# Sum of squares behind the first weight slice, and a head in another order: a float32 hybrid trunk on one core

## The chip, the cores and the metric

One core of one Trainium2 chip runs the kernel. The metric is device time in microseconds of one launch that computes both layers. The kernel before takes 2107.37 us (median of 3 runs, 2106.95 to 2107.5).

## What is computed

Each of two layers normalizes x, projects it once, mixes the columns in three branches, merges these with gates and adds a last projection to x. Cut to what matters here:

```
for i in range(DEPTH):                                  # DEPTH = 2
    h = rmsnorm(x, norm_w[i])                           # x: 256 tokens x 2048
    proj = h @ w_in[i]                                  # 2048 x 13840
    (u, s5_gate, z, xbc, dt_raw, q, k, v, att_gate, merge_logits) = split(proj)
    ...                                                 # S5, SSD and attention branches
    branches = einsum('blnw,nwd->blnd', ys, w_branch[i])
    merged = sum(sigmoid(merge_logits) * branches)
    x = x + merged @ w_out[i]

def rmsnorm(t, w):
    y = t * rsqrt(mean(t * t, axis=-1) + 1e-6)
    return y * w
```

## The kernel before, in words

x lies transposed: 16 tiles of 128 channels by 256 tokens. The scale of the norm over the channels, norm_w, is multiplied in before the projection, and the scale over the tokens, called rstd, after it, when a result leaves PSUM. So the products need the scaled x only, and rstd is first needed by the tensor operation that empties the bank of slice 0.

**Products.** All large weights come as a stream of 148 slices per layer, each 128 x 2048 float32 (1 MB). Slice n is loaded by SP into one of two buffers `raw`, rounded by ACT to `w_hi` (helper `hi`, L580), and DVE takes the rest, `w_lo` = raw - w_hi (helper `lo`, L860). x is split likewise into `h_hi` and `h_lo`. PE computes a slice as 48 products (`pair`, and three calls at L1464 to L1466: w_hi x h_lo, w_lo x h_hi, w_hi x h_hi, for 16 tiles of channels). `raw`, `w_hi`, `w_lo` and the PSUM banks `mm` have two places each: slice n + 2 can be rounded only when the products of slice n are done (semaphore `pair_done`), and slice n + 2 can be multiplied only when DVE has emptied the bank of slice n.

**Order of work.** Every engine has its own program in the order in which it is written (blocks `sync` for SP, `gpsimd` for POOL, `scalar` for ACT, `vector` for DVE, `tensor` for PE), and semaphores join them. In the head SP loads x in four quarters of 512 KB (L344), norm_w (L346), the first two slices (L348), the constants (L349), and copies x to the output (L350). ACT squares the 16 tiles (L597), POOL adds the squares up in `ssum` (L416), and DVE multiplies the tiles by norm_w (L888). Then ACT and DVE split slices 0 and 1.

**Start of a layer.** ACT makes the four quarters of `h_hi` (L606, marks xhi0 to xhi3), DVE those of `h_lo` (xlo0 to xlo3). In `first(0)` PE waits for `ssum` and multiplies it by a matrix of ones (L1502, mark "ss"), which gives the sum over the channels in bank b4; only then it starts slice 0. DVE turns b4 into mean plus eps behind xlo0 (L900, mark "rs_v"), ACT takes Ln (L590) and Exp (L592) of it (`inv_sqrt`), and DVE improves the result by one Newton step of four operations (`newton`, ending in mark "rs_n4"). Behind slice 0 PE waits for rs_n4 and transposes rstd (L1522, mark "rtok"). In the loop over n of DVE (0 to 15) each turn waits for the products of slice n, empties the bank (mark "in" and n), and splits slice n + 2. Turn 0 ends with `s5_angles`, a chain of 14 small operations, whose first needs "s5_dt" of ACT, and which ACT's Tanh (L619) waits for before it rounds slice 3. In the second layer the squares and the scaled tiles come from the loop over the slices of w_out (squares L845, sums on POOL L559, scaling L1450).

Of the kernel before, what the change touches and what calls it, by code (L numbers as in the profile page):

```python
# [10 lines left out]
ALU = mybir.AluOpType  # L11
# [13 lines left out]
EPS = 1e-6  # L25
# [107 lines left out]
def program(nc, x, norm_w, params, consts, bdense, stream, xs_out, order):  # L133

    with ExitStack() as ctx:
# [204 lines left out]

        @block.sync
        def _(e):
            for q in range(4):
                e.dma_start(proj[:, 4 * q:4 * q + 4, :], x[:, 4 * q:4 * q + 4, :]).then_inc(x_in[q], 16)  # L344
                if q == 0:
                    e.dma_start(nw[:, 0:DEPTH, :], norm_w).then_inc(nw_in, 16)  # L346
            for j in range(RAW):
                e.dma_start(raw[:, j, :], stream[j]).then_inc(landed[j], 16)  # L348
            e.dma_start(cst[:], consts).then_inc(const_in, 16)  # L349
            e.dma_start(xs_out[0], x).then_inc(x_copied, 16)  # L350
            W = Where(e)

            def load(nb, j):

                e.wait_ge(lo_done, nb + (j + 1 + RAW))
                e.dma_start(raw[:, j % RAW, :], stream[nb + (j + RAW)]).then_inc(landed[j % RAW], 16)

            with e.Fori(0, DEPTH) as L:
                with e.Fori(0, N_GATE // 2 + 1) as I:
                    nb = e.snap(L * N_LAYER + I * 2)  # L360
                    for j in range(2):
                        load(nb, j)

                with e.Fori(0, 4) as I:
                    nb = e.snap(L * N_LAYER + N_GATE + I * 12)
                    g0 = e.snap(I * 12)

                    for c in range(2):
                        W.b[MA] = e.snap((L * 8 + I * 2 + (c + 2)) * MA.n)
                        for t in range(6):  # L370
                            s = 6 * c + t
                            W.wait(MA, f"gate{t}")
                            e.dma_start(gscr[g0 + s], gt[:, s % 4, :]).then_inc(spilled[s % 4], 16)
                            load(nb, s + 2)
                with e.Fori(0, (N_BR - N_SG) // 2 - 1) as I:
                    nb = e.snap(L * N_LAYER + (N_SG + 2) + I * 2)
                    for j in range(2):
                        load(nb, j)

                for s in range(4):  # L380
                    e.wait_ge(spilled[s], e.snap((L * 12 + 13) * 16))
                W.settle()
                with e.Fori(0, (N_OUT - N_BR) // 2) as I:
                    nb = e.snap(L * N_LAYER + N_BR + I * 2)
                    for j in range(2):
                        load(nb, j)
                        e.dma_start(gin[:, j % 2], gscr.rearrange("(n a) p t -> n p a t", a=2)[I * 2 + j]).then_inc(gate_in[j % 2], 16)
                with e.Fori(0, (N_LAYER - N_OUT) // 2) as I:
                    nb = e.snap(L * N_LAYER + N_OUT + I * 2)
                    for j in range(2):  # L390
                        load(nb, j)
            e.wait_ge(x_out, (DEPTH + 1) * 64)
            e.wait_ge(x_copied, 16)
# [170 lines left out]
        def _(e):  # L564
# [29 lines left out]
            for m in range(KT):  # L594
                if m % 4 == 0:
                    e.wait_ge(x_in[m // 4], 16)
                e.activation(proj[:, 16 + m, :], proj[:, m, :], ACT.Square).then_inc(x_sq, 1)  # L597
            hi(0, 0)
            hi(0, 1)
            with e.Fori(0, DEPTH) as L:  # L600
                W.layer(L)

# [1 line left out]
                for q in range(4):  # L604
                    e.wait_ge(x_w, e.snap(L * 16 + (4 * q + 4)))
                    LA.mark(e.activation(h_hi[:, 4 * q:4 * q + 4, :], proj[:, 32 + 4 * q:36 + 4 * q, :], ACT.Copy), f"xhi{q}")  # L606
                inv_sqrt(LA, "rs", rstd[:], sv[:, 1, :], sv[:, 0, :], lambda: W.wait(LV, "rs_v"))

                nb = start(L, 0)
                for n in range(16):  # L610
                    hi(nb, n + 2)
                    if n == 0:
                        e.wait_ge(par_in, e.snap((L + 1) * 16))
                        LA.mark(e.activation(sp[:, 0, :], PR("log_dt", 0, ST), ACT.Exp), "s5_dt")
                        LA.mark(e.activation(sd[:, 6, 0:16], PR("a_log", 0, 16), ACT.Exp), "exp_a")
                        LA.mark(e.activation(wdt_hi[:], PR("w_dt", 0, KT * 16).rearrange("p (k c) -> p k c", k=KT), ACT.Copy), "wdt_hi")
                        LA.mark(e.activation(bgh[:], PR("b_glu", 0, BT), ACT.Copy, scale=0.5), "bgh")
                        W.wait(LV, "s5_ax")
                        LA.mark(e.activation(sp[:, 2, :], sp[:, 1, :], ACT.Tanh, scale=0.5), "s5_tanh")  # L619
                    if n == 1:  # L620
                        W.wait(LV, "turn_abs")
                        LA.mark(e.activation(sp[:, 5, :], sp[:, 3, :], ACT.Sin, scale=TWO_PI / 2), "s5_sin")
                        LA.mark(e.activation(sp[:, 6, :], sp[:, 4, :], ACT.Sin, scale=-TWO_PI / 2, bias=C("half_pi")), "s5_cos")
                    if n == 5:
                        W.wait(LV, "dt_abs")
                        LA.mark(e.activation(sd[:, 2, :], sd[:, 1, :], ACT.Exp, scale=-1.0), "dt_exp")
                    if n == 6:
                        W.wait(LV, "k_raw")
                        LA.mark(e.activation(kk[:, 0, :], kt[:].rearrange("p a b -> p (a b)"), ACT.Square), "k_sq")
                    if 4 <= n < 8:  # L630
                        t = n - 4
                        W.wait(LV, f"bc_conv{t}_3")
                        if t:
                            W.wait(LV, f"bc_silu{t - 1}")
                        LA.mark(e.activation(bt[:], kk[:, 2, 0:TOK] if t % 2 == 0 else kk[:, 2, TOK:], ACT.Tanh, scale=0.5), f"bc_tanh{t}")
                    if n == 8:
                        inv_sqrt(LA, "k", kk[:, 0, :], kk[:, 1, :], kk[:, 3, :], lambda: W.wait(LV, "k_v"))
                    if n == 13:
                        W.wait(LV, "k_fin")
                        e.dma_start(kscr.rearrange("a p t -> p a t"), kt[:]).then_inc(k_out, 16)  # L640
                        LA.mark(e.activation(small[:, 12:13], C("half_pi"), ACT.Copy), "prep_end")
# [208 lines left out]
        def _(e):  # L850
# [34 lines left out]
            for m in range(KT):  # L885
                if m % 4 == 0:
                    e.wait_ge(x_in[m // 4], 16)
                e.tensor_scalar(proj[:, 32 + m, :], proj[:, m, :], nw[:, 0, m:m + 1], None, ALU.mult).then_inc(x_w, 1)  # L888
            lo(0, 0)
            lo(0, 1)  # L890
            with e.Fori(0, DEPTH) as L:
                W.layer(L)
                e.wait_ge(x_w, e.snap((L + 1) * 16))
                for q in range(4):
                    W.wait(LA, f"xhi{q}")
                    LV.mark(tt_(h_lo[:, 4 * q:4 * q + 4, :], proj[:, 32 + 4 * q:36 + 4 * q, :],
                                h_hi[:, 4 * q:4 * q + 4, :].bitcast(F32), ALU.subtract), f"xlo{q}")
                    if q == 0:
                        W.wait(LP, "ss")
                        LV.mark(e.tensor_scalar(sv[:, 0, :], b4[:, 0:TOK], 1.0 / D_MODEL, EPS, ALU.mult, ALU.add), "rs_v")  # L900
                newton(LV, "rs", rstd[:], sv[:, 1, :], sv[:, 0, :])


                count = [0]

# [114 lines left out]
                for n in range(16):  # L1020
                    if n == 8:
                        e.wait_ge(x_out, e.snap((L + 1) * 64))
                        W.settle()
                    e.wait_ge(pair_done, nb + (n + 3))
                    bank = mm[:, n % 2, 0:256]
                    if n < 4:
                        LV.mark(tt_(proj[:, BC + n, :], bank, rstd[:], ALU.mult), f"in{n}")
# [9 lines left out]
                    if n == 4:  # L1037
                        W.wait(LP, "dt_t")
                        LV.mark(tt_(sv[0:16, 0, :], b6[0:16, 0:256], rstd[0:16, :], ALU.mult), "dt_s")
                    lo(nb, n + 2)  # L1040
                    if n == 0:
                        s5_angles()
                    if n == 1:
                        W.wait(LP, "rtok")
                        chain(e.tensor_copy(rtok[:], b5[:, 0:2]), "rtok")
                        W.wait(LA, "wdt_hi")
                        LV.mark(tt_(wdt_lo[:], PR("w_dt", 0, KT * 16).rearrange("p (k c) -> p k c", k=KT), wdt_hi[:].bitcast(F32),
                                    ALU.subtract), "wdt_lo")
# [407 lines left out]
        def _(e):  # L1456
# [33 lines left out]
                                    xhi[:, k, :], xlo[:, k, :], k == 0, k == BT - 1)  # L1490
                ins.then_inc(pair_done, 1)

            e.wait_ge(const_in, 16)
            with e.Fori(0, DEPTH) as L:
                W.layer(L)

                xs = e.snap(L * 17 + 18)

                def first(q):
                    if q == 0:  # L1500
                        e.wait_ge(x_sum, xs)
                        LP.mark(e.matmul(b4[:, 0:TOK], C("ones"), ssum[:], start=True, stop=True), "ss")  # L1502
                    W.wait(LV, f"xlo{q}")


                nb = e.snap(L * N_LAYER)
                for n in range(16):
                    if n in (6, 7):
                        e.wait_ge(lo_done, nb + (n + 1 + RAW))
                        for t in range(2):  # L1510
# [5 lines left out]
                    else:  # L1516
                        pair(nb, n, first if n == 0 else None)
                    if n == 0:

                        W.wait(LV, "rs_n4")  # L1520
                        for t in range(2):
# [328 lines left out]
```

## Time and profile before

| | before |
|---|---|
| median of 3 runs | 2107.37 us |
| span of the profiled execution, first to last instruction | 2106.1 us |
| what a run has around that span (difference of the two) | 1.3 us |
| TensorE matmul busy | 2024.8 us, 96% |
| VectorE busy | 1610.8 us, 76% |
| ScalarE busy | 1040.8 us, 49% |
| GpSimd busy | 669.4 us, 32% |
| mean granted TensorE clock | 0.995 of full |

The time of a run covers one launch. The profile is of one execution, and its span goes from the first instruction to the last. Busy time counts data work of an engine, not its waits. PE is the multiplying part of TensorE, PEld its loading of weights; DVE is VectorE, ACT ScalarE, POOL GpSimd, SP SyncE. A granted clock of 1.00 is 2.4 GHz, one of 0.50 is 1.2 GHz.

### The profile page before, as it was taken

Reading aid. Unit: us, or ns where it says so; the run is one execution under the profiler, and the core shown is the slowest. Engines: PE = TensorE matmul, PEld = TensorE weight load, DVE = VectorE, ACT = ScalarE, POOL = GpSimd, SP = SyncE. Lnnn points to the kernel's source line nnn. Section 1 sums busy time; section 2 is a strip of 40 time slices with the busy share of each in tenths; the row PEclk is TensorE's granted clock in tenths of the full one; section 3 lists DMA queues with packets and bytes.
Section 4 is the critical chain, followed back from the end, with each engine's and each line's share of the span. In section 5 each row is a group of like instructions: output and inputs, shape, how many; then the busy total and the mean of one; then the engine's idle time right before and its main releaser. Section 6 shows DMA issues by size and latency. Waiting matters only on the chain.

```text
span 2106.1 us, 45313 instructions
## 1 busy us (share of the span) xinstructions
PE 2024.8 (96%) x15852; PEld 1921.2 (91%) x15852; DVE 1610.8 (76%) x2366; ACT 1040.8 (49%) x1389; POOL 669.4 (32%) x816
## 2 busy tenths in 40 slices
PE   5999999999999999999989999999999999999998
PEld 5999999988888999999989899999888889999998
DVE  6658899888898867766567688889898978586755
ACT  5334334657665645333343344447565666453333
POOL 3045666434353000002300656665343330000033
PEclk9999999999999999999999999999999999999999
DMA  6344444434344445665543444444443444466654
GB/s 245 128 169 143 159 151 151 160 141 156 138 159 142 155 156 218 231 225 205 201 163 127 167 154 155 146 166 142 148 164 142 138 156 143 161 243 227 231 195 179
DMA packets 74125, 356.98 MB, mean 170 GB/s; under 512 B 8048, under 2 KB 33136, under 8 KB 35440
## 3 DMA queue, kind: packets, MB, share of 16 engines
q1 hardware_dynamic: 70704, 342.93, 45.5%
q0 software_dynamic: 1600, 7.85, 1.0%
q10 hardware_dynamic: 1696, 4.72, 0.6%
q8 instruction: 56, 0.92, 0.2%
q14 instruction: 69, 0.57, 0.1%
HBM read 338.17 MB, written 19.40 MB: 170 GB/s over the span
## 4 chain that ended last, share of the span: by engine, by line
PE 83%; DVE 6%; issue 5%; ACT 2%; POOL 2%; DVEq 0%; DMA 0%; ACTq 0%; POOLq 0%; SPq 0%
PE mm L1464 24%; PE mm L1465 23%; PE mm L1466 23%; PE bs L1569 3%; PE b L1557 3%; DVE w_lo L860 1%; DVE prod L864 1%; PE by L1624 1%; ACT w_hi L580 1%; DVE xc L1005 1%; PE b L1615 1%; PE b L1636 1%; PE b L1635 1%; POOL ssum L416 1%; PE b L1642 0%
## 5 line engine op out<-in xcount | busy, mean ns | idle before, releaser
L1464 PE MATMUL mm<-h_lo,w_hi 128*128 128x256 f32 x3776 | 1103.9, 292 | 3.5 <-DVE h_lo L864 3.5
L1465 PE MATMUL mm<-h_hi,w_lo 128*128 128x256 f32 x3776 | 1070.7, 284 | 0.0
L1466 PE MATMUL mm<-h_hi,w_hi 128*128 128x256 f32 x3776 | 1070.2, 283 | 0.0
L580 ACT ACTIVATE w_hi<-raw 128x2048 fp32r<-128x2048 f32 x298 | 569.6, 1911 | 792.1 <-PE mm L1466 775.5
L860 DVE TENSOR_TENSOR w_lo<-raw,w_hi 128x2048 fp32r<-128x2048 f32 x298 | 696.7, 2338 | 160.1 <-ACT w_hi L580 152.2
L1464 PEld LDWEIGHTS mm<-h_lo,w_hi 128*128 128x128 f32 x3776 | 725.4, 192 | 35.0 <-issue 27.4
L1465 PEld LDWEIGHTS mm<-h_hi,w_lo 128*128 128x128 f32 x3776 | 725.8, 192 | 3.9 <-issue 1.0
L1466 PEld LDWEIGHTS mm<-h_hi,w_hi 128*128 128x128 f32 x3776 | 725.3, 192 | 0.0
L1464 PE MATMUL mm<-ys,w_hi 128*128 128x256 f32 x768 | 217.5, 283 | 2.2 <-DVE w_lo L860 2.2
L1465 PE MATMUL mm<-ys,w_lo 128*128 128x256 f32 x768 | 217.3, 283 | 0.0
L1466 PE MATMUL mm<-ys,w_hi 128*128 128x256 f32 x768 | 217.3, 283 | 0.0
L559 POOL TENSOR_TENSOR ssum<-ssum,proj 128x256 f32<-128x256 f32 x32 | 72.7, 2271 | 398.3 <-ACT proj L845 398.3
L1464 PEld LDWEIGHTS mm<-ys,w_hi 128*128 128x128 f32 x768 | 147.4, 192 | 2.6 <-DVE w_lo L860 2.6
L1466 PEld LDWEIGHTS mm<-ys,w_hi 128*128 128x128 f32 x768 | 147.4, 192 | 0.0
L1465 PEld LDWEIGHTS mm<-ys,w_lo 128*128 128x128 f32 x768 | 147.4, 192 | 0.0
L864 DVE TENSOR_TENSOR prod<-prod,prod 128x256 f32<-128x256 f32 x256 | 121.8, 515 | 1.7
L437 POOL TENSOR_SCALAR tA<-cst,cur 128x256 f32<-128x256 f32 x64 | 65.3, 1021 | 148.7 <-ACT tab L651 143.5
L468 POOL COPY cz<-par 64x64 f32 x64 | 47.6, 744 | 194.2 <-PE bs L1569 185.7
L864 DVE TENSOR_TENSOR proj<-mm,rstd 128x256 f32 (+1 forms) x104 | 43.6, 419 | 74.4 <-PE mm L1466 73.5
L864 DVE TENSOR_TENSOR prod<-wst,tab 128x512 f32<-128x512 f32 x128 | 89.3, 738 | 0.5
L549 POOL DMA_DIRECT2D x_old<-out x2 | 1.2, 610 | 277.8 <-PE mm L1466 277.8
L448 POOL TENSOR_TENSOR tB<-tB,tA 128x256 f32<-128x256 f32 x64 | 85.0, 1329 | 5.3
(268 smaller groups left out, 2576.4 us busy)
## 6 DMA issues: line engine op xcount, KB each, us to landing
raw<-in_stream SPq DMA_DIRECT2D x298, 1024.0 KB, 4.8
gscr<-gt SPq DMA_DIRECT2D x96, 128.0 KB, 1.7
gin<-gscr SPq DMA_DIRECT2D x48, 256.0 KB, 4.9
x_old<-out POOLq DMA_DIRECT2D x2, 2048.0 KB, 10.6
out<-proj ACTq DMA_DIRECT2D x8, 512.0 KB, 3.7
proj<-in_x SPq DMA_DIRECT2D x4, 512.0 KB, 6.9
par<-in_params POOLq DMA_DIRECT2D x2, 759.0 KB, 5.4
cst<-in_consts SPq DMA_DIRECT2D x1, 1029.0 KB, 12.8
```

The costliest lines, as they stand in the source:

```text
L437: SGp.mark(e.tensor_scalar(tA[:], C("iota"), cur5[:, j:1 + j], ROUND, ALU.mult, ALU.add), f"ta{j}")
L448: SGp.mark(e.tensor_tensor(tB[:], tB[:], tA[:], ALU.add), f"tf{j}")
L468: SGp.mark(e.tensor_copy(cz[rows, :, r, 16 * g:16 * g + 16], par[rows, bass.ds(i * 64 + PP[nm][0], 64)].rearrange("p (j h) -> p j h", j=4) ...
L559: e.tensor_tensor(ssum[:], ssum[:], proj[:, bass.ds(I * 4 + (16 + j), 1), :].rearrange("p a b -> p (a b)"), ALU.add).then_inc(x_sum, 1)
L580: e.activation(w_hi[:, j % SPLIT, :], raw[:, j % RAW, :], ACT.Copy).then_inc(hi_done, 1)
L860: e.tensor_tensor(w_lo[:, j % SPLIT, :], raw[:, j % RAW, :], w_hi[:, j % SPLIT, :].bitcast(F32), ALU.subtract).then_inc(lo_done, 1)
L864: return e.tensor_tensor(out, a, b, op)
L1464: e.matmul(out, whi, xlo, start=start, stop=False)
L1465: e.matmul(out, wlo, xhi, start=False, stop=False)
L1466: return e.matmul(out, whi, xhi, start=False, stop=stop)
L1557: ins = e.matmul(b4[:, r * 256:r * 256 + 256], bz[:, r, 2 * j:2 * j + 2, :].rearrange("p a b -> p (a b)"), proj[:, bass.ds(I + (U + more), ...
L1569: ins = e.matmul(ps_s5[32 * j:32 * j + 32, :], cz[:, j, r, :], prod[:, j % 2, r, :], start=r == 0, stop=r == 1)
```

## The change

Four things move; no operation on data is added or dropped.

- On PE the product "ss", with its waits for the constants and for `ssum`, goes from ahead of slice 0 to behind it, and "rtok" from behind slice 0 to behind slice 1. Ahead of slice 2 PE now waits for "in0", the emptying of the bank of slice 0.
- On DVE "rs_v", the Newton step and in0 stand in turn 0 behind the split of slice 2; the copy of rtok goes from turn 1 to turn 2.
- On ACT Ln and Exp stand behind the rounding of slice 2.
- In the head SP loads norm_w first, and slices 0 and 1 behind quarters 0 and 1 of x. ACT rounds slice 0 behind tile 3 and slice 1 behind tile 7; DVE takes the rest of slice 0 behind tile 7 and of slice 1 behind tile 15.

```diff
 @block.sync
+            e.dma_start(nw[:, 0:DEPTH, :], norm_w).then_inc(nw_in, 16)
             for q in range(4):
                 e.dma_start(proj[:, 4 * q:4 * q + 4, :], x[:, 4 * q:4 * q + 4, :]).then_inc(x_in[q], 16)
-                if q == 0:
-                    e.dma_start(nw[:, 0:DEPTH, :], norm_w).then_inc(nw_in, 16)
-            for j in range(RAW):
-                e.dma_start(raw[:, j, :], stream[j]).then_inc(landed[j], 16)
+                if q < RAW:
+                    e.dma_start(raw[:, q, :], stream[q]).then_inc(landed[q], 16)
 @block.scalar
                 e.activation(proj[:, 16 + m, :], proj[:, m, :], ACT.Square).then_inc(x_sq, 1)
-            hi(0, 0)
-            hi(0, 1)
+                if m == 3:
+                    hi(0, 0)
+                if m == 7:
+                    hi(0, 1)
...
-                inv_sqrt(LA, "rs", rstd[:], sv[:, 1, :], sv[:, 0, :], lambda: W.wait(LV, "rs_v"))
                 for n in range(16):
                     hi(nb, n + 2)
                     if n == 0:
+                        inv_sqrt(LA, "rs", rstd[:], sv[:, 1, :], sv[:, 0, :], lambda: W.wait(LV, "rs_v"))
                         e.wait_ge(par_in, e.snap((L + 1) * 16))
 @block.vector
                 e.tensor_scalar(proj[:, 32 + m, :], proj[:, m, :], nw[:, 0, m:m + 1], None, ALU.mult).then_inc(x_w, 1)
-            lo(0, 0)
+                if m == 7:
+                    lo(0, 0)
             lo(0, 1)
...
-                    if q == 0:
-                        W.wait(LP, "ss")
-                        LV.mark(e.tensor_scalar(sv[:, 0, :], b4[:, 0:TOK], 1.0 / D_MODEL, EPS, ALU.mult, ALU.add), "rs_v")
-                newton(LV, "rs", rstd[:], sv[:, 1, :], sv[:, 0, :])
...
                     e.wait_ge(pair_done, nb + (n + 3))
+                    if n == 0:
+                        lo(nb, n + 2)
+                        W.wait(LP, "ss")
+                        LV.mark(e.tensor_scalar(sv[:, 0, :], b4[:, 0:TOK], 1.0 / D_MODEL, EPS, ALU.mult, ALU.add), "rs_v")
+                        newton(LV, "rs", rstd[:], sv[:, 1, :], sv[:, 0, :])
...
-                    lo(nb, n + 2)
+                    if n:
+                        lo(nb, n + 2)
                     if n == 0:
                         s5_angles()
-                    if n == 1:
+                    if n == 2:
                         W.wait(LP, "rtok")
                         chain(e.tensor_copy(rtok[:], b5[:, 0:2]), "rtok")
+                    if n == 1:
                         W.wait(LA, "wdt_hi")
 @block.tensor
-            e.wait_ge(const_in, 16)
...
                 def first(q):
-                    if q == 0:
-                        e.wait_ge(x_sum, xs)
-                        LP.mark(e.matmul(b4[:, 0:TOK], C("ones"), ssum[:], start=True, stop=True), "ss")
                     W.wait(LV, f"xlo{q}")
                 for n in range(16):
+                    if n == 2:
+                        W.wait(LV, "in0")
...
                     if n == 0:
+                        e.wait_ge(const_in, 16)
+                        e.wait_ge(x_sum, xs)
+                        LP.mark(e.matmul(b4[:, 0:TOK], C("ones"), ssum[:], start=True, stop=True), "ss")
+                    if n == 1:
                         W.wait(LV, "rs_n4")
```

How the instructions stand now: the start of a layer on ACT before, from the last quarter of h_hi (L606) to the rounding of slice 2 (L580). L590 is Ln and L592 Exp, each behind a table load.

```order
L606 ACTIVATE h_hi<-proj 128x1024
L331 ISA
L590 ACT_TABLE_LOAD
L590 ACTIVATE sv<-sv 128x256
L331 ISA
L592 ACT_TABLE_LOAD
L592 ACTIVATE rstd<-sv 128x256
L578 ISA
L579 REGISTER_ALU
L580 ACTIVATE w_hi<-raw 128x2048
```

The same place on ACT in the changed kernel, whose lines are L607, L579, L589 and L591:

```order
L607 ACTIVATE h_hi<-proj 128x1024
L577 ISA
L578 REGISTER_ALU
L579 ACTIVATE w_hi<-raw 128x2048
L331 ISA
L589 ACT_TABLE_LOAD
L589 ACTIVATE sv<-sv 128x256
L331 ISA
L591 ACT_TABLE_LOAD
L591 ACTIVATE rstd<-sv 128x256
```

The rounding of slice 2 now stands ahead of Ln, both table loads and Exp.

The same place on DVE in the changed kernel, from the last quarter of h_lo to the emptying of the bank of slice 0. L861 is the rest of slice 2, L1025 is rs_v, the four rows behind it are the Newton step, and the last is in0.

```order
L865 TENSOR_TENSOR h_lo<-proj,h_hi 128x1024
L1021 ISA
L861 TENSOR_TENSOR w_lo<-raw,w_hi 128x2048
L331 ISA
L1025 TENSOR_SCALAR sv<-b 128x256
L331 REGISTER_ALU
L865 TENSOR_TENSOR sv<-rstd 128x256
...
L865 TENSOR_TENSOR sv<-sv 128x256
...
L877 TENSOR_SCALAR sv<-sv 128x256
...
L865 TENSOR_TENSOR rstd<-rstd,sv 128x256
...
L865 TENSOR_TENSOR proj<-mm,rstd 128x256
```

Before, rs_v stood behind the first quarter of h_lo, the Newton step behind the last, then in0, and the rest of slice 2 last.

## Rows read from the trace of the kernel before

**Rows 1.** The page, part 1: an engine's busy us, share, instructions.

```profile
PE 2024.8 (96%) x15852; PEld 1921.2 (91%) x15852; DVE 1610.8 (76%) x2366; ACT 1040.8 (49%) x1389; POOL 669.4 (32%) x816
```

**Rows 2.** Waits of PE over the span: us in total, times, longest us.

```profile
PE b L1502 <- POOL ssum L416: 25.3, 1, 25.3
...
PE b L1676 <- DVE xc L1284: 10.1, 6, 2.0
PE b L1557 <- POOL bz L460: 5.8, 2, 2.9
PE b L1502 <- POOL ssum L559: 4.9, 1, 4.9
```

**Rows 3.** Head: SP's issues (start us, us), then the last quarter's transfer (us to landing).

```profile
1.79 1.38 SPq L344 DMA_DIRECT2D proj<-in_x  x3
```

```profile
proj<-in_x SPq DMA_DIRECT2D x1, 512.0 KB, 8.1
```

**Rows 4.** Timeline of ACT, 27 to 40 us: start us, us, instruction.

```profile
27.42 1.28 ACT L592 ACT_TABLE_LOAD   x1
28.72 0.42 ACT L592 ACTIVATE rstd<-sv 128x256 f32<-128x256 f32 x1
33.33 1.91 ACT L580 ACTIVATE w_hi<-raw 128x2048 fp32r<-128x2048 f32 x1 [4.20 <-PE mm L1466]
...
39.53 1.91 ACT L580 ACTIVATE w_hi<-raw 128x2048 fp32r<-128x2048 f32 x1 [1.59 <-PE mm L1466]
```

**Rows 5.** Timeline of DVE, 8 to 41 us.

```profile
8.30 5.59 DVE L888 TENSOR_SCALAR proj<-proj,nw 128x256 f32<-128x256 f32 x12 [1.27 <-DMA proj<-in_x]
...
20.29 1.74 DVE L864 TENSOR_TENSOR h_lo<-proj,h_hi 128x1024 fp32r<-128x1024 f32 x1
26.53 0.43 DVE L900 TENSOR_SCALAR sv<-b 128x256 f32<-128x256 f32 x1 [4.49 <-PE b L1502]
...
30.27 0.42 DVE L864 TENSOR_TENSOR sv<-rstd 128x256 f32<-128x256 f32 x1
...
31.51 0.42 DVE L864 TENSOR_TENSOR rstd<-rstd,sv 128x256 f32<-128x256 f32 x1
...
35.28 2.29 DVE L860 TENSOR_TENSOR w_lo<-raw,w_hi 128x2048 fp32r<-128x2048 f32 x1 [1.52 <-ACT w_hi L580]
37.49 0.41 DVE L864 TENSOR_TENSOR sp<-par,sp 128x32 f32<-128x32 f32 x2
...
40.50 0.42 DVE L864 TENSOR_TENSOR proj<-mm,rstd 128x256 f32<-128x256 f32 x1
```

**Rows 6.** POOL: all 16 adds of the head, and one beside w_lo.

```profile
5.73 19.49 POOL L416 TENSOR_TENSOR ssum<-ssum,proj 128x256 f32<-128x256 f32 x16 [4.11 <-ACT proj L597]
```

```profile
15.49 2.72 POOL L416 TENSOR_TENSOR ssum<-ssum,proj 128x256 f32<-128x256 f32 x1
```

**Rows 7.** Timeline of PE around slice 0; last, a product of the chain (start, us).

```profile
25.27 1.22 PE L1502 MATMUL b<-ssum,cst 128*128 128x256 f32 x2 [25.27 <-POOL ssum L416]
25.93 0.78 PE L1464 MATMUL mm<-h_lo,w_hi 128*128 128x256 f32 x1
...
33.13 0.50 PE L1522 MATMUL b<-cst,rstd 128*128 128x1 f32 x4
```

```profile
28.84 0.14 PE mm L1466
```

**Rows 8.** Start of the second layer, timelines of ACT and PE.

```profile
1064.49 3.90 ACT L606 ACTIVATE h_hi<-proj 128x1024 fp32r<-128x1024 f32 x4 [4.12 <-issue]
```

```profile
1066.86 0.58 PE L1464 MATMUL mm<-h_lo,w_hi 128*128 128x256 f32 x1 [2.61 <-DVE h_lo L864]
...
1069.58 0.39 PE L1464 MATMUL mm<-h_lo,w_hi 128*128 128x256 f32 x1
```

**Rows 9.** Stretches: us, PE busy (instructions), granted clock, DMA share, GB/s.

```profile
148.50:151.50 3.00, 3.00 (x14) 0.50 0.19 27
476.00:479.00 3.00, 3.00 (x16) 0.50 0.71 300
```

## The prediction, made before the changed kernel was run

> **What bounds the kernel now.** The page's first part shows PE busy for 2024.8 of 2106.1 us [rows 1], so only what makes PE idle, or multiply slowly, can change the time by much. I therefore read PE's waits next. The longest is the start: PE sits for 25.3 us until POOL has summed the squares of the first layer, and at the second layer it waits 4.9 us for the same sum [rows 2]. Then I read the timelines of the head and of the boundary between the layers, engine by engine, to see what else would hold slice 0 if that sum did not. In the head DVE had the first quarter of h_lo at 22.03 us (20.29 + 1.74) [rows 5], so 3.9 us of the wait up to 25.93, where slice 0 starts [rows 7], are the sum's. At the second layer slice 0 starts at 1066.86 and was released by h_lo, itself held by ACT, which began h_hi only at 1064.49 behind 4.1 us that are put down to issue [rows 8]. There the wait for the sum is covered: ss could vanish and slice 0 would start no earlier.
>
> **Term 1, the head.** In the new order 2.0 MB have to land before quarter 1 of x is there (quarter 0, slice 0, quarter 1). The same 2.0 MB were the four quarters before; the last was issued at about 2.7 (the end of 1.79 + 1.38, less its own 0.4) and landed 8.1 later, at 10.8 [rows 3]. From there DVE is busy without a gap. Its scaling takes 5.59 / 12 = 0.47 us a tile beside POOL's adds, w_lo 2.29, the first quarter of h_lo 1.74 [rows 5]: 4 x 0.47 + 2.29 + 8 x 0.47 + 2.29 + 1.74 = 11.95, less some 0.25 where neighbours overlap, gives 22.5. ACT keeps ahead of it: a rounding takes 1.91 [rows 4], and by my count slice 0, whose data are in with the first 1.5 MB, is rounded by about 11.5, and slice 1 by about 15.4. So the new order of the head brings nothing by itself, slice 0 can start at 22.5 instead of 25.93, and all that is won is the wait for the sum.
>
> A part of it is lost again. Of what PE did from 25.27 until 28.84 everything ran slowly, one product in 0.21 us, and 0.12 from then on [rows 7]. The product ss, some 1.2 us, no longer takes the first part of these 3.6 us, so slice 0 has about 17 slow products instead of 11: its products take 17 x 0.21 + 31 x 0.12 = 7.3 us, 7.5 with the filling of the pipe, and slice 0 ends at 30.0. It ended at 33.3 (ACT is released at 33.33, [rows 4]). **Gain 3.3 us.** From below I take 2.3 (each of the two w_lo and the quarter held 0.3 longer by POOL), from above 4.8: the four scalings between transfers at 0.35 each, and quarter 1 a microsecond earlier.
>
> Is the sum ready when slice 0 ends? POOL took 19.49 us for 16 adds, and one beside w_lo took 2.72 [rows 6]. In the new order it does 4 by about 10, waits for the next squares until 11.9, and has four long adds beside two w_lo and four quarters of h_lo: I come to 28.5, under 30.0. If it is later by up to 2 us nothing follows, as the next term shows.
>
> **Term 2, the stall before slice 2, in each layer.** This is what the change adds. Let slice 0 end at 0. Before, slice 2 followed at 39.53 - 33.33 = 6.2 [rows 4]: rtok and slice 1, whose bank and weights were ready. Now its bank must be emptied by in0, and in0 stands at the end of a chain that starts with the rounding of slice 2. Step by step, each with its duration: the rounding 1.91; w_lo of slice 2 starts 1.95 behind the rounding's start (35.28 against 33.33) and the next operation 2.21 behind that [rows 4, 5], so rs_v starts at 4.2 and ends at 4.6, while ss (0.6 us at the full clock) is long done; Ln takes 0.43, and table load and Exp 29.14 - 27.42 = 1.72 [rows 4], to 6.8; the table load for Ln stands ahead of its wait and hides behind w_lo; the Newton step takes 31.93 - 30.27 = 1.66 [rows 5], to 8.5; in0 0.42, to 8.95; the first product starts at 9.1 with its pipe empty. PE meanwhile has ss and slice 1, 6.4 us, then sits for 2.1, does rtok (0.35) when rs_n4 is there, and sits again. So slice 2 starts 9.1 - 6.2 = **2.9 us later, in each layer**. What is queued behind the wait is only slice 2 itself, so the delay passes on whole.
>
> Here a row and a rule differ. Exp starts 1.30 us behind the start of its table load, with nothing between [rows 4]. The Trainium skill (ScalarE: Activation LUTs, What ACT_TABLE_LOAD costs) puts every change of table at 2.66 us, load and drain; with that the chain would be 1.4 us longer in each layer. The row decides; the rule is a rival below.
>
> What is late next: DVE does s5_angles behind in0, 3.0 us (37.49 to 40.50), and only then in1 and w_lo of slice 3 [rows 5]. That gives 8.95 + 3.0 + 0.4 + 2.3 = 14.65, and slice 2 ends at 9.1 + 5.76 = 14.9. So slice 3 is not held, by 0.2 us.
>
> **Term 3, the second layer.** Slice 0 starts at 1066.86 as before, since h_lo is what it waits for. Its products were slow until about 1069.8, 2.9 us [rows 8]; without ss at 1063 that can be as in the head, up to 3.6, which costs 0 to 0.35. I take **0.1 us**.
>
> **Term 4, the clock.** The stalls of term 2 can also cost clock. PE's two waits of some 2.9 us for bz were both followed by about 3.4 us at 0.50 (148.5 to 151.5 shows the first). Of the six waits for xc, of up to 2.0 us, one was: behind it PE stood at 0.50 in 476 to 479, and did 16 products in 3 us [rows 2, 9]. That costs 3.4 / 2 = 1.7 us each time. My stalls have 2.1 us without work, rtok, and 0.25 more, between these cases. Six in ten each, I estimate; so one fall in two stalls is likeliest: **1.7 us**.
>
> The rest costs nothing: the load of norm_w ahead of x is 0.4 us of issue inside the transfers that quarter 1 waits for; the constants' transfer is long in; rtok's copy moved to turn 2 is 0.15 us on DVE, with slice 6 its first reader.
>
> **Sum.** -3.3 + 2 x 2.9 + 0.1 + 1.7 = +4.3 us on the profiled 2106.1. The median of the runs is 1.3 above that span and takes the same difference: 2107.4 + 4.3 = 2111.7. A difference of under 0.2%, 4.2 us, is what measurement can't tell from none, so the forecast sits on the edge of it.
>
> **Rivals.**
> - The clock falls in neither stall: +2.6, 2110.0, no measurable change. For it: five of six waits of about 1.5 to 2.0 us left the clock alone. Against: the stall is nearer 2.5.
> - It falls in both: +6.0, 2113.4. The two stalls are alike, and so were the two for bz, which both fell.
> - The head wins more, 4.8 us, with stalls of 2.8 and no fall: +0.8 + 0.1, 2108.3. For it: transfers could land earlier in another order. Against: DVE has 12 us of work in a row that no transfer holds. To come out faster at all, the head has to win 5.9, thus slice 0 has to start before 20; nothing of DVE's rows allows that.
> - The chain of term 2 is longer than its operations, by 1.4 us a layer: an engine that changes its table waits for its pipe to drain. Then slice 2 is 4.3 late, and the time 4.3 + 2.8 = +7.1, 2114.5. This is what the rule above would make of it. Against: the 1.30 us of the row.
> - The change does not do what it says, in that PE waits for the sum all the same: ssum later than slice 0's end by over 2.1 us, thus past 32. Each microsecond beyond adds one. It needs three more long adds than I count.
>
> **How the numbers follow.** Forecast (one fall) 0.42; none 0.19; both 0.28; the head wins more 0.06; the longer chain 0.02; the late sum 0.03. Each has some 1.5 us of its own, from the phase of the clock, from fetches of instructions (the 4.1 us put down to issue may move), and from terms 1 and 2. So above +4.2 lie half of the first, an eighth of the second, nearly all of the third and the last two: slower 0.52. Below -4.2 almost nothing: 0.02. Within 0.2%: 0.46. The range goes from +0.4, which takes in the rival of the head, to +8.0: 2107.8 to 2115.4.
>
> **What would show it.** In the changed profile: slice 0 starts at 22 to 23 us without a wait for ssum; POOL's last add ends before 30; ahead of rtok, and again ahead of slice 2, PE waits for DVE's rstd and proj, 2 to 2.7 us together in each layer; slice 2 starts 9.1 us behind the end of slice 0 in place of 6.2; slice 0 of the second layer starts at h_lo, 2.61 us of wait with ss gone becoming a long one; a granted clock of 0.50 for 3.4 us behind one of the stalls. A slice 0 that starts before 21, or a stall under 1.5 us, would make the prediction wrong.

## The result, and the profile after

The changed kernel takes 2113.84 us (median of 6 runs, 2113.38 to 2114.55) against 2107.40 before (6 runs): ratio 1.0032, 95% interval 1.0022 to 1.0042. It is slower by 6.4 us, of which 4.3 were forecast. The profiled execution has a span of 2112.3 us, 6.2 above that of before.

The page, part 1, and PE's waits of the changed kernel answer to [rows 1, 2]:

```profile
PE 2029.7 (96%) x15852; PEld 1926.7 (91%) x15852; DVE 1611.0 (76%) x2366; ACT 1040.4 (49%) x1389; POOL 670.4 (32%) x816
```

```profile
PE mm L1468 <- DVE h_lo L865: 31.4, 4, 21.8
...
PE b L1683 <- DVE xc L1288: 10.1, 6, 1.9
PE b L1564 <- POOL bz L459: 5.7, 2, 2.8
PE b L1529 <- DVE rstd L865: 4.5, 2, 2.5
```

PE has the same 15852 instructions and is busy for 4.9 us more: slower products, not more of them. The two waits for ssum of 25.3 and 4.9 us are gone, waits for h_lo stand in their place, 21.8 us at the start and 8.7 at the second layer, and new are two for DVE's rstd, 4.5 us together. What follows are the timelines of ACT, DVE and PE around the first two slices [rows 4, 5, 7]:

```profile
29.14 1.91 ACT L579 ACTIVATE w_hi<-raw 128x2048 fp32r<-128x2048 f32 x1 [8.50 <-PE mm L1470]
31.07 1.28 ACT L589 ACT_TABLE_LOAD   x1
33.82 0.42 ACT L589 ACTIVATE sv<-sv 128x256 f32<-128x256 f32 x1 [1.46 <-DVE sv L1025]
34.25 1.28 ACT L591 ACT_TABLE_LOAD   x1
35.55 0.42 ACT L591 ACTIVATE rstd<-sv 128x256 f32<-128x256 f32 x1
...
45.81 1.92 ACT L579 ACTIVATE w_hi<-raw 128x2048 fp32r<-128x2048 f32 x1 [3.77 <-PE mm L1470]
```

```profile
10.01 1.14 DVE L889 TENSOR_SCALAR proj<-proj,nw 128x256 f32<-128x256 f32 x4 [2.23 <-DMA proj<-in_x]
...
20.04 6.77 DVE L865 TENSOR_TENSOR h_lo<-proj,h_hi 128x1024 fp32r<-128x1024 f32 x4
31.16 2.29 DVE L861 TENSOR_TENSOR w_lo<-raw,w_hi 128x2048 fp32r<-128x2048 f32 x1 [4.34 <-ACT w_hi L579]
33.37 0.42 DVE L1025 TENSOR_SCALAR sv<-b 128x256 f32<-128x256 f32 x1
35.99 0.43 DVE L865 TENSOR_TENSOR sv<-rstd 128x256 f32<-128x256 f32 x1 [2.21 <-ACT rstd L591]
...
37.24 0.43 DVE L865 TENSOR_TENSOR rstd<-rstd,sv 128x256 f32<-128x256 f32 x1
37.70 0.42 DVE L865 TENSOR_TENSOR proj<-mm,rstd 128x256 f32<-128x256 f32 x1
```

```profile
21.84 0.58 PE L1468 MATMUL mm<-h_lo,w_hi 128*128 128x256 f32 x1 [21.84 <-DVE h_lo L865]
...
37.72 0.61 PE L1529 MATMUL b<-cst,rstd 128*128 128x1 f32 x4 [2.04 <-DVE rstd L865]
38.26 0.51 PE L1468 MATMUL mm<-h_lo,w_hi 128*128 128x256 f32 x1
```

The chain is to be read from top to bottom: PE frees slice 0's weights at 29.14, the rounding, the rest of slice 2 and the mean follow, Ln waits for the mean, Exp for its table, and rstd and in0 come at 37.67 and 38.12. Slice 2 starts at 38.26, 9.12 us behind the end of slice 0. Before, its first product was this one, 6.00 behind that end (33.33):

```profile
39.33 0.28 PE L1464 MATMUL mm<-h_lo,w_hi 128*128 128x256 f32 x1
```

The second layer of the changed kernel, and the clock behind both stalls:

```profile
1075.56 1.92 ACT L579 ACTIVATE w_hi<-raw 128x2048 fp32r<-128x2048 f32 x1 [6.92 <-PE mm L1470]
...
1092.22 1.91 ACT L579 ACTIVATE w_hi<-raw 128x2048 fp32r<-128x2048 f32 x1 [3.74 <-PE mm L1470]
```

```profile
1067.10 0.58 PE L1468 MATMUL mm<-h_lo,w_hi 128*128 128x256 f32 x1 [8.73 <-DVE h_lo L865]
```

```profile
38.50:41.50 3.00, 3.00 (x15) 0.50 0.02 5
1086.00:1089.00 3.00, 3.00 (x18) 0.54 0.01 3
```

Columns as in [rows 9]: PE was busy throughout both stretches and did 15 and 18 products in 3 us, where 25 fit at the full clock.

Where the 6.2 us of the two spans lie, by the moments at which ACT is released to round the slice behind the next (the end of slice 0 and of slice 2):

| stretch | before | after | difference |
|---|---|---|---|
| start to end of slice 0 | 33.33 | 29.14 | -4.2 |
| end of slice 0 to end of slice 2 | 11.96 | 16.67 | +4.7 |
| on to slice 0 of layer 2 | 1021.57 | 1021.29 | -0.3 |
| slice 0 of layer 2 | 7.33 | 8.46 | +1.1 |
| end of slice 0 to end of slice 2 | 11.96 | 16.66 | +4.7 |
| on to the end | 1019.95 | 1020.08 | +0.1 |

Each +4.7 has two parts. Slice 2 starts 9.12 us behind the end of slice 0 in place of 6.00, which is 3.1 of stall. From its first product to ACT's release it then takes 7.55 us (38.26 to 45.81) in place of 5.96 (39.33 to 45.29), which is 1.6, nearly all of it the slow clock: the kernel below in which the clock stays takes 6.06.

### The profile page after: what moved, and what is told of

Read it like the earlier page. It is cut to its first block, busy times and chain, and to the rows that moved or that the text cites. A ratio compares the mean times of both kernels' runs of the same rounds, so it can differ in the third digit from the quotient of the medians.

```text
span 2112.3 us, 45317 instructions
## 1 busy us (share of the span) xinstructions
PE 2029.7 (96%) x15852; PEld 1926.7 (91%) x15852; DVE 1611.0 (76%) x2366; ACT 1040.4 (49%) x1389; POOL 670.4 (32%) x816
## 3 DMA queue, kind: packets, MB, share of 16 engines
q0 software_dynamic: 1600, 7.85, 1.0%
## 4 chain that ended last, share of the span: by engine, by line
PE 81%; DVE 7%; issue 6%; ACT 3%; POOL 1%; DMA 1%; DVEq 0%; ACTq 0%; POOLq 0%; SPq 0%
PE mm L1468 24%; PE mm L1469 23%; PE mm L1470 23%; PE bs L1576 3%; PE b L1564 3%; DVE w_lo L861 2%; DVE prod L865 1%; ACT w_hi L579 1%; PE by L1631 1%; DVE xc L1002 1%; PE b L1622 1%; PE b L1643 1%; PE b L1642 1%; PE b L1649 0%; DMA proj<-in_x 0%
## 5 line engine op out<-in xcount | busy, mean ns | idle before, releaser
L579 ACT ACTIVATE w_hi<-raw 128x2048 fp32r<-128x2048 f32 x298 | 569.6, 1911 | 801.3 <-PE mm L1470 788.9
L861 DVE TENSOR_TENSOR w_lo<-raw,w_hi 128x2048 fp32r<-128x2048 f32 x298 | 697.4, 2340 | 164.7 <-ACT w_hi L579 157.5
```

Of the source, the lines that this page charges most:

```text
L579: e.activation(w_hi[:, j % SPLIT, :], raw[:, j % RAW, :], ACT.Copy).then_inc(hi_done, 1)
L861: e.tensor_tensor(w_lo[:, j % SPLIT, :], raw[:, j % RAW, :], w_hi[:, j % SPLIT, :].bitcast(F32), ALU.subtract).then_inc(lo_done, 1)
```

## The experiments

Ten kernels ran, on three chips, and on each chip the kernel before as well. It took 2106.96 us beside the two parts, the filled stall and the early table; 2106.16 beside the early mean and the three kernels with 12 products; and 2106.35 beside the one with 18 and the unaltered change. Times are medians of their runs. Kernels of different chips are compared by their distance to the kernel before on their own chip; that of the change is +6.4 us.

**The two parts apart.** The first has the new head alone: the load of norm_w and of slices 0 and 1, and the three splits, as in the change, with all else as before. The second is the whole change with the head undone:

```diff
-            e.dma_start(nw[:, 0:DEPTH, :], norm_w).then_inc(nw_in, 16)
             for q in range(4):
                 e.dma_start(proj[:, 4 * q:4 * q + 4, :], x[:, 4 * q:4 * q + 4, :]).then_inc(x_in[q], 16)
-                if q < RAW:
-                    e.dma_start(raw[:, q, :], stream[q]).then_inc(landed[q], 16)
+                if q == 0:
+                    e.dma_start(nw[:, 0:DEPTH, :], norm_w).then_inc(nw_in, 16)
+            for j in range(RAW):
+                e.dma_start(raw[:, j, :], stream[j]).then_inc(landed[j], 16)
...
-                if m == 3:
-                    hi(0, 0)
-                if m == 7:
-                    hi(0, 1)
+            hi(0, 0)
+            hi(0, 1)
...
-                if m == 7:
-                    lo(0, 0)
+            lo(0, 0)
```

> Only the head's new order; the product of the sum of squares stays ahead of slice 0. Theory (the new head wins nothing by itself, all is the wait for the sum): POOL gets its later squares later, so the sum is ready at about 26 us in place of 25.2 and slice 0 starts with it: 2108.3, 0 to 2 us above before. Rival (the new head is worth the 4 us by which slice 0 came earlier): slice 0 starts before 24 us, 2105 or less.

> Only the moved product, with all that was moved with it; the head in the old order. Theory: slice 0 starts at the first quarter of h_lo, at about 22.1 us, so nearly where the whole change has it (21.8), the two stalls ahead of slice 2 and both falls of the clock are there, and the time is that of the whole change within 1 us, 2114. Rival (the head's order carries a part of the gain): 2116 or more.

Measured: 2108.45 us for the head alone, ratio 1.0010 (1.0001 to 1.0019), and 2113.88 for the moved product alone, 1.0037 (1.0024 to 1.0051). PE's first instruction in each, by the timeline:

```profile
26.68 1.22 PE L1504 MATMUL b<-ssum,cst 128*128 128x256 f32 x2 [26.68 <-POOL ssum L415]
```

```profile
22.62 0.58 PE L1466 MATMUL mm<-h_lo,w_hi 128*128 128x256 f32 x1 [22.62 <-DVE h_lo L864]
```

With the new head the sum comes 1.4 us later (25.27 before), since POOL gets the squares later. Behind the moved product the new head makes slice 0 start 0.8 us earlier (21.84 against 22.62). Against the kernel before on their chip these are +1.5 us for the head and +6.9 for the moved product, where the whole change has +6.4. Both theories hold: the loss belongs to the moved product and what was moved with it, and the head alone loses 1.5.

**The clock's share.** The change, and three products of constants into an unused bank behind slice 1:

```diff
                     if n == 1:
+                        for _ in range(3):
+                            e.matmul(b7[:, 0:TOK], C("ones"), C("tri"), start=True, stop=True)
                         W.wait(LV, "rs_n4")
```

> The whole change, and three products of constants behind slice 1, whose result nobody reads, some 0.6 us each, inside the 2.0 us in which PE waits for rstd. Theory (each stall costs 2.9 us by its chain and 1.7 to 1.8 more by the clock that falls behind it): the chain stays, slice 2 starts where it did, no granted clock of 0.50 behind it; 3.5 us under the whole change, 2110.3. Rival (the slow stretch costs nothing, or the clock falls anyway): within 1 us of the whole change, 2113.8.

Measured: 2108.87 us, ratio 1.0012 (1.0003 to 1.0021). PE's timeline and the clock at the place where the change had 0.50:

```profile
35.84 1.46 PE L1528 MATMUL b<-cst 128*128 128x256 f32 x6
38.45 0.61 PE L1531 MATMUL b<-cst,rstd 128*128 128x1 f32 x4 [1.15 <-DVE rstd L865]
38.98 0.38 PE L1468 MATMUL mm<-h_lo,w_hi 128*128 128x256 f32 x1
```

```profile
38.00:41.00 3.00, 2.55 (x21) 1.00 0.18 71
```

Slice 2 still starts 9.1 us behind the end of slice 0 (29.86 in this run), so the chain is as long as it was, but the clock stays at 1.00, each product takes its 0.12 us, and slice 2 ends 15.18 behind slice 0 in place of 16.67: 1.5 us less in each layer. So the clock's share is shown, at 3.0 us for both. The kernel is 1.9 above its kernel before, 4.5 less than the change has and more than the 3.5 forecast. What goes beyond 3.0 can't be put down to the filling. In its profile two falls of the clock are missing that the change had far behind the stalls, at 1195 and 1618, and the one at 1195 is missing behind a wait for bz that is as long as ever:

```profile
1191.17 0.48 PE L1566 MATMUL b<-proj,bz 128*128 x1 [2.85 <-POOL bz L459]
```

Such falls come and go from one execution to the next (below), and the runs of this kernel spread from 2106.0 to 2111.7. Leaving out the last 6 to 7 us of each span, time at 0.50 (twice what the mean granted clock of each stretch of 5 us lacks to 1.00, times 5) adds up to 17.0 us before, 30.6 with the change and 13.7 here. Some of it is idle time and costs nothing.

**The chain's share.** Two kernels shorten it, with PE's order as in the change. In the first, DVE does rs_v ahead of the rest of slice 2. In the second, besides that, ACT loads the table of Ln before it rounds slice 2:

```diff
                     if n == 0:
-                        lo(nb, n + 2)
                         W.wait(LP, "ss")
                         LV.mark(e.tensor_scalar(sv[:, 0, :], b4[:, 0:TOK], 1.0 / D_MODEL, EPS, ALU.mult, ALU.add), "rs_v")
+                        lo(nb, n + 2)
                         newton(LV, "rs", rstd[:], sv[:, 1, :], sv[:, 0, :])
```

```diff
+                e.wait_ge(const_in, 16)
+                e.activation(small[:, 13:14], C("eps"), ACT.Ln)
                 nb = start(L, 0)
                 for n in range(16):
                     hi(nb, n + 2)
```

> The whole change with one step of the chain moved: DVE does the mean (rs_v) ahead of the rest of slice 2; ACT as in the change, so it still loads the table of Ln behind the rounding. Theory: rounding 1.95, table load to 3.25, Ln to 3.7, table load and Exp to 5.4, Newton step to 7.1, in0 to 7.5: slice 2 starts at 7.6 behind the end of slice 0 in place of 9.1, PE sits for 0.7 and 0.3 us, and the clock stays. 1.45 + 1.8 us less in each layer, 6.4 in all: 2107.4. Rival (the clock falls at any stall): 2.9 less, 2110.9.

> The whole change with a shorter chain: DVE does the mean (rs_v) ahead of the rest of slice 2, and ACT loads the table of Ln ahead of the rounding of slice 2, by a Ln of one column of constants whose result nobody reads. Theory: from the end of slice 0 rounding 1.95, Ln 0.43, table load and Exp 1.72, rest of slice 2 until 4.25, Newton step to 5.9, in0 6.35: slice 2 starts at 6.5, right behind slice 1, no stall and no fall of the clock. 2.6 + 1.8 us less in each layer, 8.6 in all: 2105.2, under both kernels. Rival (something else than this chain holds slice 2, such as the new wait itself): less than 4 us gained, 2110 or more.

Measured: 2106.85 us for the first, ratio 1.0001 (0.9992 to 1.0010), and 2104.52 for the second, 0.9990 (0.9981 to 0.9999). In the first, PE waits 1.00 us for rstd, and slice 2 starts 7.67 behind the end of slice 0 (30.82):

```profile
37.96 0.61 PE L1529 MATMUL b<-cst,rstd 128*128 128x1 f32 x4 [1.00 <-DVE rstd L865]
38.49 0.38 PE L1468 MATMUL mm<-h_lo,w_hi 128*128 128x256 f32 x1
```

The granted clock is 1.00 in every us from there to 45.5. ACT's timeline in the second:

```profile
29.39 1.91 ACT L579 ACTIVATE w_hi<-raw 128x2048 fp32r<-128x2048 f32 x1 [7.33 <-PE mm L1472]
31.21 0.40 ACT L589 ACTIVATE sv<-sv 128x256 f32<-128x256 f32 x1
...
32.92 0.42 ACT L591 ACTIVATE rstd<-sv 128x256 f32<-128x256 f32 x1
35.94 1.90 ACT L579 ACTIVATE w_hi<-raw 128x2048 fp32r<-128x2048 f32 x1
41.86 1.91 ACT L579 ACTIVATE w_hi<-raw 128x2048 fp32r<-128x2048 f32 x1 [2.26 <-PE mm L1472]
```

Ln follows the rounding at once, and Exp ends 3.95 us behind the end of slice 0 in place of 6.83. The end of slice 2 (41.86) stands 12.47 behind that of slice 0 where the change had 16.67 and the kernel before 11.96: both the stall and the slow stretch are gone, in each layer. PE's wait for rstd stands nowhere in its list any more. So the new wait for in0 is not what costs; the length of what in0 waits for is. Both theories hold within 1 us: against the kernel before they forecast 0.0 and -2.2 us, and +0.7 and -2.4 were measured.

**The second layer's start.** Its slice 0 took 8.5 us in the change and 7.3 before, and PE has nothing to do for 8.7 us ahead of it. These kernels give it products of constants at the end of a layer: 12 on the change, 12 on the short chain, 12 there and 3 more ahead of the first layer, and last 18 on the short chain.

```diff
                     for j in range(4):
                         pair(nb, j, (lambda q: e.wait_ge(merged_lo, e.snap(L * KT + (4 * q + 4)))) if j == 0 else None)
+                for _ in range(12):
+                    e.matmul(b7[:, 0:TOK], C("ones"), C("tri"), start=True, stop=True)
```

> The whole change, and 12 products of constants behind the last slice of each layer, some 0.6 us each, in the time in which PE waits for the second layer's h_lo; nobody reads them, and behind the second layer they lie beside the last output's way out. Theory (without the product ss PE has nothing to do for 8.7 us, and slice 0 of the second layer is slow for over 4 us, 8.5 in place of 7.3 before): slice 0 of the second layer takes 5.9, 2.5 us less in all: 2111.3. Rival (the slow start comes from the engine's restart, not from its idle time): 8.5 as it was, 2113.8.

> The short chain of e5_table_early and the 12 products at the end of each layer. Theory: slice 0 of the second layer falls from 7.85 to 5.9 us, and no stall follows: 2104.5 - 1.9 = 2102.6. Rival (the 12 products get in the way of slice 0 or of the end): 2104.5 or more.

> As e8_early_warm, and 3 such products ahead of the first layer, behind the constants at about 17.5 us. Theory: slice 0 of the first layer falls from 7.65 to some 6 us and ends at 27.8, but POOL has the sum of squares only at about 29.2, so the product ss, and slice 1 behind it, wait for it, and nearly all of that gain is lost: 2102.4, within 0.7 of e8_early_warm. Rival (slice 0's slow start is worth its 1.7 us in full): 2100.9.

> As e8_early_warm with 18 products in place of 12: in that run one took 0.44 us, so 12 ended 3.8 us ahead of slice 0 of the second layer, and the clock fell all the same. 18 take 8.0 and leave 1.1 us. Theory (the clock falls with the idle time): slice 0 of the second layer takes 5.9 us, none of it at 0.50; 2103.0 - 1.6 = 2101.4. Rival (the clock falls there whatever PE does): 7.5 us, 2103.0.

| kernel | median us | ratio to before, interval | slice 0 of layer 2 |
|---|---|---|---|
| 12 on the change | 2113.06 | 1.0029, 1.0018 to 1.0041 | 7.6 |
| 12 on the short chain | 2102.97 | 0.9986, 0.9977 to 0.9995 | 7.5 |
| the same, 3 ahead of layer 1 | 2105.45 | 0.9993, 0.9984 to 1.0002 | 8.8 |
| 18 on the short chain | 2101.25 | 0.9975, 0.9964 to 0.9985 | 6.1 |

Twelve were too few. On the change they gained nothing (+6.9 us against the kernel before, where the change has +6.4), and the expectation of 5.9 us for slice 0 failed in both kernels that had them. The time of the second, 2102.97, is near the 2102.6 forecast, but not for the reason given: slice 0 lost 0.3 us of its 7.85, and its profile lacks a fall of the clock behind the second wait for bz, at 1185. One product took 0.44 us and not 0.6, and PE's timeline with 12 on the change shows 3.8 us left to wait, the one with 18 on the short chain 1.3; ACT's release below it gives the end of that slice 0:

```profile
1057.80 5.34 PE L1748 MATMUL b<-cst 128*128 128x256 f32 x24
1066.92 0.38 PE L1468 MATMUL mm<-h_lo,w_hi 128*128 128x256 f32 x1 [3.77 <-DVE h_lo L865]
```

```profile
1053.35 7.93 PE L1750 MATMUL b<-cst 128*128 128x256 f32 x36
1062.58 0.39 PE L1470 MATMUL mm<-h_lo,w_hi 128*128 128x256 f32 x1 [1.29 <-DVE h_lo L867]
```

```profile
1068.64 1.92 ACT L579 ACTIVATE w_hi<-raw 128x2048 fp32r<-128x2048 f32 x1 [3.01 <-PE mm L1472]
```

With 1.3 us of wait the clock stayed, slice 0 took 6.1 us, and the kernel comes to 2101.25, 5.1 us below the kernel before on its chip. The restart of the engine is not the cause; its idle time is.

The products ahead of the first layer show the other expectation of that row. PE's timeline there:

```profile
17.86 2.93 PE L1501 MATMUL b<-cst 128*128 128x256 f32 x6 [17.86 <-DMA cst<-in_consts]
21.79 0.39 PE L1470 MATMUL mm<-h_lo,w_hi 128*128 128x256 f32 x1 [1.00 <-DVE h_lo L867]
...
29.15 0.70 PE L1529 MATMUL b<-ssum,cst 128*128 128x256 f32 x2 [0.65 <-POOL ssum L415]
29.49 0.47 PE L1470 MATMUL mm<-h_lo,w_hi 128*128 128x256 f32 x1
```

Slice 0 ended at 28.5, 1.2 earlier than in the same kernel without them (29.7), but ss waited until 29.15 for POOL, as expected; slice 2 started 0.3 us earlier, and by the second layer nothing of it was left (the 12 products start at 1053.53 with them and at 1053.51 without). That the run is 2.5 us slower was not expected. Its profiled execution, the slowest of the eleven, has slice 0 of layer 2 at 8.8 in place of 7.5, and 3.4 us of wait at 1876, behind a weight slice that landed late, where the other has 1.1. Why its median lies higher stays open; no run was made for it.

**Once more.** The changed kernel, unaltered:

> The changed kernel once more, unaltered, to see how far its slow stretches move from one execution to the next. Theory (when the clock falls and rises again is a matter of the moment, not of the product ss): slice 0 of the second layer takes another time than 8.46 us, between 7.2 and 8.8, and the falls behind far waits (for bz, for xc) stand elsewhere, while slice 2 starts 9.0 behind the end of slice 0 in both layers again: 2113.8 within 1. Rival (the 8.46 us come from the missing ss): 8.4 to 8.5 again.

Measured: 2113.44 us, ratio 1.0027 (1.0017 to 1.0037). In its profiled execution slice 2 starts 9.1 behind the end of slice 0 again, while slice 0 of the second layer takes 7.74 us, from

```profile
1067.46 0.58 PE L1468 MATMUL mm<-h_lo,w_hi 128*128 128x256 f32 x1 [8.72 <-DVE h_lo L865]
```

to ACT's release at 1075.20. The stretches at 0.50 far behind lie elsewhere as well: at 672, 1522 and 1717 here, at 1618 in the first profile. With the head alone, where ss does stand at 1063, that slice took 7.84, and with the moved product alone, without ss, 7.40. So the missing ss alone does not make it 8.46; a small share is not excluded, since the two profiles with ss have 7.33 and 7.84 and the six with neither ss nor filling products there 7.40 to 8.46.

**What the length of a wait says of the clock.** In four profiles PE waits for over 2 us for rstd ahead of slice 2, with nothing to fill the stall: two of the change, one of the moved product alone and one of 12 products on the change. Over all twelve profiles, with the kernel before, PE's waits and the granted clock in the 5 us behind each come to this:

| PE waits for | us | waits | with a clock of 0.50 behind them |
|---|---|---|---|
| bz | 2.8 to 3.0 | 24 | 21 |
| rstd, ahead of slice 2 | 2.0 to 2.5 | 8 | 8 |
| xc | 1.79 to 1.99 | 14 | 7 |
| xc | 1.4 to 1.78 | 51 | 0 |

The three waits for bz without a fall are those of the second layer in the filled stall and in two kernels with 12 products, the one on the short chain and the one with 3 more. A wait of the same length can do either, so a single fall says little on one kernel.

## Why the prediction was right, point by point

The time lies in the range (2107.8 to 2115.4) and on the forecast side. The likeliest case was one fall of the clock; the rival with both is what came, 2113.4 forecast and 2113.84 measured. That these two agree so well is in part luck: the head won 0.9 us more than its term, and the second layer cost 1.0 more than its own.

- **Term 1, the head.** Forecast -3.3, measured -4.2. Slice 0 started at 21.84, not 22.5: quarter 1 landed at 10.0 and not 10.8, and its four scalings took 1.14 together and not 1.9 (POOL was waiting for squares). Most of that was lost again: DVE then waited 0.42 us for quarter 2, although the prediction has it busy without a gap, and the second w_lo took 2.81 and not 2.29. Slice 0 took 7.30 us in place of 7.5. The statement behind the term stands by test: the head alone gives no gain.
- **The sum in time.** Forecast 28.5; POOL's last add ended at 29.17 in the changed kernel and ss ran at 29.22, 0.1 behind the end of slice 0. It was nearer to a wait than the 1.5 us I had, and the kernel with products ahead of layer 1 ran into it.
- **Term 2, the stalls.** Forecast 9.1 us to slice 2 and 2.9 late, in each layer. Measured 9.1, and 3.1 late. Every step of the chain took its time of the rows within 0.1. The 0.2 are a misreading: 6.2 was the time to the end of slice 1, at which ACT is released, and the first product of slice 2 had started 0.2 ahead of that, at 39.33. Exp starts 1.30 behind its table load (34.25, 35.55), so the rule of the Trainium skill (ScalarE: Activation LUTs, What ACT_TABLE_LOAD costs), by which the drain would make it 1.4 us more, does not agree with this trace.
- **Slice 3.** Forecast to be ready 0.2 us ahead. In the change w_lo of slice 3 ended at 43.54, 14.4 behind the end of slice 0, and slice 2 took until 45.81, so it was ready. With the stall filled and the clock full it was ready as well, by 0.8: at 44.28, against 45.04.
- **Term 3, the second layer.** Forecast +0.1, and +1.1 in the profile. This is a term that was mis-sized, and my reason for it was wrong too. I took the slow part of slice 0 to be 3.6 us at most, as in the head; the granted clock was 0.50 for the first 5.5 us here. In eleven of the twelve profiles that slice takes 7.3 to 8.8 us, wherever PE has sat idle for over 2 us ahead of it, with or without ss; only the kernel with 18 products has 6.1.
- **Term 4, the clock.** Forecast one fall in two stalls, at 1.7 us. Both fell, in all four profiles with such stalls, and in the change each cost 1.6. This is the step that went wrong: I put a stall's chance at six in ten from waits of other lengths, and made one fall of two the likeliest although the prediction itself calls the two stalls alike. Eight of eight fell. The price was near, but its working is off: 3.4 us at 0.50 do not cost half of that, since a product takes 0.21 us at 0.50 and 0.12 at 1.00, so they cost 1.5.
- **The sum.** For the profiled executions: -4.2 for the head, 6.2 for the stalls, 3.2 for the clock behind them, 1.1 for the second layer and -0.15 for the rest make the +6.2 measured, where -3.3, 5.8, 1.7 and 0.1 made +4.3.

## What to carry to other kernels

Moving a wait off the start of a chain is worth only what its consumer's new place leaves: here 4.2 us were won once, and 3.1 of stall and 1.6 of slow clock were paid in each layer, because the operations that release slice 2 were put behind the splitting of slice 2. When a product moves behind other work, list everything between it and its first reader on every engine, and start that list early: the mean ahead of the long subtraction, and the table load ahead of the rounding, turned the loss of 6.4 us into a gain of 2.4. A stall on TensorE can cost more than its length: here a stall of 3.1 us came to 4.7, since the clock fell behind it.

## What the runs showed of the hardware that I had not expected

- Three products that nobody needs, 1.46 us in all, inside a stall that stays as long as it was, kept the clock at 1.00 and took 1.5 us off each layer.
- Behind the same 8.7 us of idle time the granted clock of the same kernel stayed at 0.50 for 5.5 us in one execution and for 3.8 in another, so the same slice took 8.46 and 7.74 us. When the clock rises again is not fixed by the kernel alone.
- POOL's adds and DVE's subtractions, both with two inputs from SBUF, hold each other up: four quarters of h_lo took 6.77 us in the head of the changed kernel and 4.63 in its second layer, where POOL was idle. POOL's last 12 adds took 18.15 us in that head, and 15.67 in the kernel with the head alone, where DVE does only the first quarter beside them.
